# First weight block of the down phase loaded straight to its place, accumulators loaded in halves

## What is computed

```python
D_FF = 2816
h = rmsnorm(x, norm2_g)
x = x + (jax.nn.silu(h @ w_gate) * (h @ w_up)) @ w_down
return rmsnorm(x, normf_g)
```

## Time and profile before

| | us |
|---|---|
| median of 3 runs | 2721.11 |
| lowest, highest | 2720.22, 2721.46 |
| the profiled execution | 2715.68 |
| span of its trace | 2713.9 |
| granted clock of TensorE, mean | 0.98 |

### The profile page before, as it was taken

The page is one execution under the profiler, slowest core; times in us unless marked ns, Lnnn a source line. Parts: engine busy times, 40 slices in busy tenths (PEclk is TensorE's granted clock), DMA queues, the critical chain, the costliest instruction groups (busy, mean ns, idle before and its releaser), DMA issues.

```text
span 2713.9 us, 32579 instructions
## 1 busy us (share of the span) xinstructions
PE 2582.8 (95%) x11600; PEld 2130.0 (78%) x11600; DVE 1571.5 (58%) x2511; ACT 893.2 (33%) x1596; POOL 134.2 (5%) x196
## 2 busy tenths in 40 slices
PE   7999789999799999989999989999996999999998
PEld 6888677888678888878888878888874888888887
DVE  4221275444476767777776686676763554455665
ACT  4333224333343333343333343333332222323333
POOL 1435400000000000000000000000000000000000
PEclk9999899999899999999999999999998999999999
DMA  3213324465732223243232252232238443453553
GB/s 149 109 74 143 141 99 147 170 229 205 273 118 101 97 92 116 102 181 116 103 113 88 101 209 89 101 116 100 96 132 322 171 141 132 143 182 121 180 208 147
DMA packets 129983, 383.77 MB, mean 141 GB/s; under 512 B 10096, under 2 KB 15728, under 8 KB 120688
## 3 DMA queue, kind: packets, MB, share of 16 engines
q1 hardware_dynamic: 125232, 365.95, 37.3%
q0 software_dynamic: 4672, 16.78, 1.6%
HBM read 256.07 MB, written 126.62 MB: 141 GB/s over the span
## 4 chain that ended last, share of the span: by engine, by line
PE 67%; DVE 3%; DMA 1%; SPq 1%; issue 0%; ACT 0%; DVEq 0%; ACTq 0%
PE bank1a L190 3%; PE bank1a L191 3%; PE bank1a L192 3%; PE bank0c L190 3%; PE bank0c L191 3%; PE bank0c L192 3%; PE bank1c L191 3%; PE bank1c L190 3%; PE bank1c L192 3%; PE bank0d L191 3%; PE bank0d L190 3%; PE bank0d L192 3%; PE bank1d L191 3%; PE bank1d L190 3%; PE bank1d L192 3%; PE bank0a L190 3%
## 5 line engine op out<-in xcount | busy, mean ns | idle before, releaser
L1607 ACT ACTIVATE w_hi<-t_raw 128x512 fp32r<-128x512 f32 x264 | 166.8, 632 | 484.0 <-PE bank0d L192 119.1
L1877 DVE TENSOR_TENSOR s_lo<-s_raw,s_hi 128x512 fp32r<-128x512 f32 x231 | 155.7, 687 | 264.0 <-ACT s_hi L1666 263.9
L1666 ACT ACTIVATE s_hi<-s_raw 128x512 fp32r<-128x512 f32 x231 | 132.9, 619 | 355.4 <-DMA s_raw<-s_scr 355.4
L1761 DVE TENSOR_TENSOR w_lo<-t_raw,w_hi 128x512 fp32r<-128x512 f32 x264 | 181.7, 688 | 36.4 <-ACT w_hi L1607 32.3
L1761 DVE TENSOR_TENSOR w_lo<-w_raw,w_hi 128x512 fp32r<-128x512 f32 x198 | 136.3, 688 | 97.8 <-ACT w_hi L1607 97.8
L1607 ACT ACTIVATE w_hi<-w_raw 128x512 fp32r<-128x512 f32 x198 | 123.9, 626 | 135.9 <-PE bank0c L192 75.0
L190 PE MATMUL z_ps<-h_hi,win_hi 128*128 128x512 f32 x384 | 153.2, 399 | 5.1 <-ACT z_out L411 5.1
L190 PE MATMUL o_ps<-wout_hi,y_hi 128*128 128x512 f32 x384 | 152.1, 396 | 3.7 <-DVE wout_lo L1236 3.7
L191 PE MATMUL z_ps<-h_lo,win_hi 128*128 128x512 f32 x384 | 150.7, 392 | 0.0
L192 PE MATMUL z_ps<-h_hi,win_lo 128*128 128x512 f32 x384 | 150.4, 392 | 0.0
L192 PE MATMUL o_ps<-wout_hi,y_lo 128*128 128x512 f32 x384 | 150.2, 391 | 0.0
(11 more groups left out here) (251 smaller groups left out, 6519.4 us busy)
## 6 DMA issues: line engine op xcount, KB each, us to landing
s_scr<-sums_out SPq DMA_DIRECT2D x33, 1792.0 KB, 6.2
s_raw<-s_scr SPq DMA_DIRECT2D x42, 1024.0 KB, 5.0
w_raw<-in_w_gate SPq DMA_DIRECT2D x66, 512.0 KB, 3.6
w_raw<-in_w_up SPq DMA_DIRECT2D x66, 512.0 KB, 4.4
wd_staged<-in_w_down SPq DMA_DIRECT2D x132, 256.0 KB
a_raw<-ha_scr SPq DMA_DIRECT2D x21, 1024.0 KB, 4.8
s_raw<-s_scr SPq DMA_DIRECT2D x21, 768.0 KB, 4.2
x<-in_x SPq DMA_DIRECT2D x24, 512.0 KB, 6.7
```

Source lines behind the costliest of these rows:

```text
L1607: act.activation(w_hi[:, j, :], src, ACT.Copy).then_inc(w_hi_done, 1)
L1666: act.activation(s_hi[c][:, k - 4 * c, :], s_raw[c][:, k - 4 * c, :], ACT.Copy).then_inc(s_hi_done, 1)
L1761: dve.tensor_tensor(w_lo[:, j, :], src, w_hi[:, j, :].bitcast(F32), ALU.subtract).then_inc(w_ready, 1)
L1877: dve.tensor_tensor(s_lo[c][:, k - 4 * c, :], s_raw[c][:, k - 4 * c, :], s_hi[c][:, k - 4 * c, :].bitcast(F32), ALU.subtract).then_inc(s_r ...
```

## The change

- **Order of the passes.** The pass of the single block (1, 1) comes first, the others keep their order. The slots of `sums_out` follow: `A22` is now slot 2, and slots 0, 1 and 3 hold other sums, with as many instructions as before.
- **Straight loading.** In the first pass the weights don't go through the stages. `load_first(0)` loads tile 0 to `t_first`, which lies where `t_lo[0]` will be; `load_first(1)` to `load_first(5)` load two tiles each (512 KB) to the places of their `t_lo`. `add_t` is gone there: ScalarE rounds from that place, and VectorE writes `t_lo` over the raw values. The places are free as the last tile's products end.
- **SP's queue at the seam** is written anew. `wd_staged` is first used by the second pass.
- **Accumulators** are loaded by GpSimd's queue, in six halves of 2 MB (`load_acc`), one for each product from the seam on, and `gain_f` with them. The third waits for the last store of the sums, whose buffer it overwrites.
- **At the turn of a token block** `make_sums` comes behind the last three `rest_of_a` instead of ahead of them.

```diff
     PASSES = (
+        ((1, 1), None, ((0, 0, ALU.subtract), (0, 1, ALU.add))),
         ((0, 0, 1, 1), ALU.add, ((0, 0, ALU.add), (1, 1, ALU.add))),
         ((1, 0, 0, 0), ALU.subtract, ((0, 0, ALU.add), (1, 0, ALU.add))),
         ((1, 0, 1, 1), ALU.add, ((0, 0, ALU.add),)),
-        ((1, 1), None, ((0, 0, ALU.subtract), (0, 1, ALU.add))),
...
-    A22, A11 = 1, 4
+    A22, A11 = 2, 4
...
+        t_first = sb("t_first", [P, HALF], F32, t_pairs[0] + K1)
+        t_raw_pairs = [sb(f"t_raw2_pair{k}", [P, 2, 2, HALF], F32, t_pairs[k]) for k in range(1, NK, 2)]
+        t_raws = [t_first[:, :]] + [pair[:, e, 1, :] for pair in t_raw_pairs for e in range(2)]
...
+            load_first(0)
             sp.wait_ge(w_ready, 7 * TILES)
-            for n in range(STAGES):
-                load_staged(n)
             sp.wait_ge(sums_stored, (NK * NB - 1) * DMA)
             load_s(0, 0)
-            sp.wait_ge(p_ready, 7 * (TILES - 1) + 4)
+            last = 7 * (TILES - 1)
+            sp.wait_ge(p_ready, last + 1)
+            load_first(1)
+            load_first(2)
+            sp.wait_ge(p_ready, last + 2)
+            load_first(3)
+            load_first(4)
+            sp.wait_ge(p_ready, last + 3)
             load_s(0, 1)
-            sp.wait_ge(p_ready, 7 * (TILES - 1) + 5)
+            load_first(5)
+            sp.wait_ge(p_ready, last + 4)
             load_s(0, 2)
-            for n in range(STAGES, STAGES + 2):
-                load_staged(n)
             store_sums(NB - 1, NK - 1, NK * NB - 1)
-            for n in range(STAGES + 2, STAGES + 5):
-                load_staged(n)
...
-            for b in range(NB):
...
-                sp.dma_start(acc[b][:, :, :],
-                             x1_scr[b * BLOCK:(b + 1) * BLOCK, :].rearrange("(t p) n -> p t n", p=P)).then_inc(acc_loaded[b], DMA)
...
-            sp.dma_start(gain_f[:, :], gf.partition_broadcast(P)).then_inc(gain_f_loaded, DMA)
...
+            def load_acc(b, half):
+                src = x1_scr[b * BLOCK:(b + 1) * BLOCK, :].rearrange("(q h p) n -> h p q n", h=2, p=P)[half]
+                pool.dma_start(acc[b][:, half::2, :], src).then_inc(acc_loaded[b][half], DMA)
...
+            pool.wait_ge(p_ready, 7 * TILES)
+            load_acc(0, 0)
+            pool.wait_ge(step_done, NK)
+            load_acc(1, 0)
+            pool.wait_ge(sums_stored, NK * NB * DMA)
+            pool.wait_ge(step_done, NK + 5)
+            load_acc(2, 0)
+            pool.wait_ge(step_done, 2 * NK)
+            load_acc(0, 1)
+            pool.dma_start(gain_f[:, :], gf.partition_broadcast(P)).then_inc(gain_f_loaded, DMA)
+            pool.wait_ge(step_done, 3 * NK)
+            load_acc(1, 1)
+            pool.wait_ge(step_done, 4 * NK)
+            load_acc(2, 1)
...
-                if e == 1:
-                    make_sums(n)
                 if turn:
                     for s in range(4, 7):
                         rest_of_a(b + 1, s)
+                if e == 1:
+                    make_sums(n)
...
-                if i == 0 and t == 0 and a == 0:
-                    dve.wait_ge(acc_loaded[b], DMA)
+                if i < 2 and t == 0 and a == i:
+                    dve.wait_ge(acc_loaded[b][i], DMA)
```

56 lines of the change are left out of this document (29 added, 27 removed).

## The result

| | before | after |
|---|---|---|
| median of the runs, us | 2721.28 (4 runs) | 2692.83 (4 runs) |
| lowest, highest | 2720.22, 2723.09 | 2688.33, 2695.33 |
| the profiled execution | 2715.68 | 2694.37 |
| span of its trace | 2713.9 | 2692.6 |

The ratio is 0.9893, interval 0.9876 to 0.9910: the change makes the kernel 1.1% faster. The forecast was 2684.8 with a range of 2681 to 2692, so the direction was right and the time 8.0 us more than forecast, just outside the range.

The account below looks back on a forecast made before the run. PE, busy 95% of the span, was taken as the bound, so only its waits and slow clock at the seam could go: 5.11 + 28.38 + 2.86 = 36.35 us, 2721.11 to 2684.8 us, range 2681 to 2692.

Parts of the forecast that it names:

- The sum of the seam: From the last tile through product 1 of the down phase: removing PE's waits and slow clock saves 36.35 us.
- Three terms: Last tile's sixth and seventh product 5.11 us, product 0 with the wait behind it 28.38, product 1 2.86.
- `u4`: Last tile: ready between 2028.3 and 2030.2, PE asks at 2030.89; no wait, margin 0.7 to 2.6 us.
- the first pair of weights: Last tile: 512 KB queued behind the first chunk of `s`, landing between 2025.0 and 2026.9.
- Rival A: Last tile: `u4` late after all, PE waits, at most the 5.11 us of the first term; 2690 us, chance 0.14.
- Accumulators ... Even 33 costs nothing: Down phase: 2 MB halves land in 12 to 33 us, wanted 30 us or more after issue; no cost.
- the chunks of product 1: Issued at 2047.3, needed at 2066.5; 8.4 us at worst, doubled by sharing with half an accumulator 17, still hidden.
- The term of the passes: Passes two to seven: 11 more joins of 0.69 us and 11 more pieces, VectorE busy 54%; costs nothing.
- the distance of 5.4 us between profile and median: Whole kernel: the runs' median lies 5.4 us above the profiled execution, and the forecast keeps that distance.
- Rival B: Product 0: weights land at half the slow rate, step 9 or 10 waits, 10.4 us come back; 2695 us, chance 0.05.
- Rival D: Down phase: halves on GpSimd's queue too late, PE waits from a landing time of 44 us on; slower, chance 0.03.
- Rival C: Seam: halves crowd chunks as before, only SP's blocked issuing goes, 10.06 and 5.3 us; 2706 us, chance 0.03.

Follow-up runs that it names:

- first_late: Changed kernel with only the second half of block 0's accumulator moved, from the start of product 2 to step 6 of product 3: 2684.95 us, ratio 0.9876.
- spread: Changed kernel with the last three accumulator halves moved to step 4 of product 3, start and step 6 of product 4, gain row last: 2682.28 us, ratio 0.9867.
- all_at_once: Changed kernel with all six halves unspaced on GpSimd's queue from the end of the last tile, third pair after the last sums' store, then gain row: 2683.50 us, 0.9858.
- after_again: The changed kernel run again, unchanged: 2688.86 us, ratio 0.9897 to the kernel before.
- halves_on_sp: Changed kernel with the same six halves and gain row at the same steps, but issued by SP between the passes' loads: 2689.06 us, ratio 0.9871.
- first_only: Kernel before plus the new first pass; six halves and gain row on SP's queue right behind the last sums' store: 2704.88 us, ratio 0.9943.

## Why the prediction was right, and where it failed

**The sum of the seam: right.** Three terms made 36.35 us. Where nothing else was lost, as in first_late, the touched part is 516.3 - 479.7 = 36.6 us shorter, and the whole span is 2677.6, which is what the prediction gave for the span. Term by term, in the kernel after: the last tile's two products take 5.98 us for a forecast 5.47, products 0 and 1 take 30.1 each, as forecast. The price of a slow clock behind a wait, taken from the earlier trace rows as part of each term, held.

**`u4`: right, with nothing to spare in one execution.** The prediction let the first pair of weights land 1.3 to 3.2 us behind the first chunk. From the timeline of ScalarE after the change:

```profile
2031.86 0.63 ACT L1692 ACTIVATE s_hi<-s_raw 128x512 fp32r<-128x512 f32 x1 [2.39 <-DMA s_raw<-s_scr]
2036.07 0.63 ACT L1700 ACTIVATE t_hi<-t_raw_pair 128x512 fp32r<-128x512 f32 x1 [3.58 <-DMA t_raw_pair<-in_w_down]
```

and from that of SP's queue:

```profile
2026.97 0.33 SPq L1550 DMA_DIRECT2D s_raw<-s_scr  x1
2028.35 4.00 SPq L1528 DMA_DIRECT2D t_raw_pair<-in_w_down  x4
```

The chunk lands 4.9 us after its issue, as forecast, the pair 4.2 us behind it, one more than the slow end of the range (3.0 to 3.6 in spread, all_at_once and first_late). PE's sixth product shows what was left of the margin of 0.7 to 2.6 us:

```profile
2039.50 0.47 PE L190 MATMUL bank1c<-a_hi,w_hi 128*128 128x512 f32 x1 [0.26 <-DVE u L1817]
```

0.26 us of wait, and none in after_again and the other kernels with the new first pass. Rival A's mechanism showed in one execution, its price didn't.

**The step that failed: "Accumulators ... Even 33 costs nothing".** The prediction priced the halves by when they are wanted themselves, and found a lead of 30 us. It didn't ask what they do to others. It did ask that once, for the chunks of product 1 ("doubled it is 17, still hidden"), and stopped there, though three more halves were put beside products 2, 3 and 4. In product 2 the first joined pass is loaded, through three stages only, and SP's queue holds the chunks of `s` behind these pieces. The term of the passes, also put at nothing, held for their own work: with no half beside them they take 30.1. It named only VectorE's 54%, though, and not the slack of their loads. The earlier trace rows showed that PE has no gap when nothing else moves 2 MB beside the chain; they didn't show how much slack the chain has.

Worked out from the start of product 2, in the kernel before: the chunk goes out at 28.8, lands in 6.1, and needs 1.4 us of rounding and subtracting, so it is ready at 36.3; PE asks at 30.1 + 11.0 = 41.1. That is a slack of 4.8 us. In after it goes out at 32.7 and lands in 10.6, 3.9 and 4.5 later, together 3.6 more than there is, and the wait is 3.4. Not all of it is the halves' doing: in spread, without one near it, the chunk goes out at 29.4 and lands in 8.0, so 2.3 us of slack are left, and the two halves take 3.3 at the issue and 2.6 in the landing. With the slow clock behind it, the wait cost 6.3 of the 8.0 us.

**The other 1.7 us** are 0.5 in the last tile, in the profiled execution, and otherwise within what an execution adds of its own: the prediction took the distance of 5.4 us between profile and median as fixed. The stage "mix" alone varies by 5.4 us. The range went 4 us below the forecast and 7 above; 2 us of the upper side were meant for that.

**Rival B** (weights of product 0 late) didn't happen, product 0 took 30.1 in every kernel with the new pass. **Rival D** (halves on GpSimd's queue too late) didn't either: they land in 8.0 to 12.5 us in after, where it needed 44, and even 34.0 in all_at_once cost nothing, as the prediction said of 33. No wait of VectorE in after ends on a load of `acc`, and the same halves issued by SP (halves_on_sp) land no sooner, in 7.3 to 13.7 us with the same median of 9.3. So GpSimd's transfers weren't held up by VectorE, busy 12 to 18 us of 30 in these products. The Trainium skill, page "SBUF — State Buffer", section "SBUF: two separate sides", names a single-source copy as what can shut GpSimd out; the trace agrees in so far as the two-source operations of this phase did no such thing.

**Rival C** (only issue time is saved, 2706) is the interesting one. Its counter-argument, that the bytes are spread over a longer time, isn't why it fell: in all_at_once nothing is spread, and the DMA engines are nearly full, as its window from 2036 to 2066 shows (columns as above; the share in the next 30 us is 0.89):

```profile
2036.00:2066.00 30.00, 30.00 (x133) 24.70 (x132) 18.45 (x30) 9.45 (x18) 2.99 (x4) 1.00 0.90 348
```

It is still 21.4 us faster than the same transfers on SP's queue. In first_only, SP's blocked issuing (18.29 + 6.23 us) lets the first chunk of product 1 go out 19.7 us late, and it then lands 12.7 us later than the usual 4.9; its slack was 12.5, and 19.9 us of wait are left. In all_at_once only the 19.7 us are gone, and there is no wait. The Trainium skill, page "DMA: Bandwidth & Descriptors", section "Issuing engines are not separate DMA queues", says that another queue saves only the issuing. The runs agree: the landing stayed at 16 to 18 us, and the time won is that of the issue. What was wrong in the rival is its price: it took 15.4 us of blocked issuing as the whole gain, and didn't ask whether the chunks, issued that much earlier, would still be waited for.

**What stays open:** why the pair of weights takes 4.2 us for 512 KB, why the chunk takes 8.0 us and not 6.1 with the new first pass, how the engines share time between two queues (no run took a half alone beside a chunk alone), and what starts the slow clock in "mix".

## What to carry to other kernels

When bulk loads are moved, list for each of them every load that it will now travel beside, to the end of the bulk, and ask of each what slack it has; the chain of three stages had little here, and each landing that was late delayed the issue of the next. Put urgent loads on a queue where no bulk stands ahead of them; after that, spreading the bulk brought nothing here, and spreading it badly cost 6 us. The two versions with later or with earlier halves (`spread` and `all_at_once`, two groups each: 2682.28 to 2683.79 us, ratios 0.9858 to 0.9871) beat the kernel before, and the kernel after by some 7 us in the touched part of their traces.

## What was not expected of the hardware

- A 2 MB load beside a chain of 256 KB loads through three stages makes eight of these take 13.2 to 13.6 us instead of 9.04. The share of the DMA engines averaged over product 2 is only 0.77; in the 12 us of the 2 MB load it is 0.97. The average hid the crowding.
- A load of 1 MB that went out 2.1 us behind one of 2 MB landed after 10.6 us, against 8.0 for the same chunk with no such load beside it, and 8.1 where the 2 MB followed it by 1.3.
- The same program can spend 143.9 or 149.3 us in the same 650 matmuls, with a granted clock of 0.92 or 0.85. A difference of 5 us between two profiles of this kernel says nothing until the untouched stages were compared.
